# Expert blocks that finish their tokens themselves: the groups dealt in turn, rows added and scattered by slot

## The reference, cut to what matters

```
xn2 = rmsnorm(x, ffn_norm_w)                      # (1088, 1024)
grp = argmax(xn2 @ w_rg + b_rg)                   # one of 4 groups for each token
e   = (xn2 @ w_re + b_re)[grp]                    # 8 experts of that group
top_v, top_i = top_k(e, 2)                        # two experts, both of the one group
top_w = softmax(top_v) * softmax(group logits)[grp]
y = x + sum over the two of  top_w * ((silu(xn2 @ w_gate[e]) * (xn2 @ w_up[e])) @ w_down[e])
```

## Time and profile before

| | |
|---|---|
| median of three runs | 1497.39 us |
| profiled execution, span from first to last instruction | 1493.6 us |
| PE, DVE, ACT, POOL busy in the span | 95%, 67%, 49%, 14% |
| block loop, from the first turn of x to the last down product | 865.6 to 1455.6 us |
| one step of the loop | 18.02 us |
| tail, from the last down product to the end | 38 us |
| moved by DMA | 347.40 MB, 394 GB/s within the loop |

### The profile page before, as it was taken

How to read it: one execution, slowest core, us unless ns; L and a number is a source line. 1 busy time by engine, 2 the same in 40 slices (tenths; PEclk the granted TensorE clock), 3 DMA queues, 4 the chain that set the end, 5 groups by cost and what they waited for, 6 DMA issues and landing times.

```text
span 1493.6 us, 21566 instructions
## 1 busy us (share of the span) xinstructions
PE 1415.8 (95%) x8064; PEld 1198.3 (80%) x8064; DVE 1001.7 (67%) x1342; ACT 726.6 (49%) x862; POOL 210.4 (14%) x243
## 2 busy tenths in 40 slices
PE   7999999999999998999999889999999999999990
PEld 7899999989999998899888666777777777777760
DVE  4422321167666667776566688888888888888875
ACT  6421121144444445423211157777777777777760
POOL 2600000021111111000200040231111111111024
PEclk9999999999999999999999799999999999999995
DMA  6346323244333324658721389999999999999948
GB/s 200 120 152 212 119 80 70 75 136 129 122 115 112 109 68 119 196 172 251 284 83 42 133 325 380 374 378 400 392 389 395 389 388 397 396 396 395 363 137 310
DMA packets 135911, 347.40 MB, mean 233 GB/s; under 512 B 13784, under 2 KB 92060, under 8 KB 110176
## 3 DMA queue, kind: packets, MB, share of 16 engines
q1 hardware_dynamic: 125688, 312.32, 58.0%
q0 software_dynamic: 6048, 21.50, 4.7%
q10 hardware_dynamic: 4120, 12.85, 2.2%
HBM read 292.34 MB, written 55.28 MB: 233 GB/s over the span
## 4 chain that ended last, share of the span: by engine, by line
PE 45%; DVE 3%; DMA 2%; ACT 1%; POOL 1%; issue 1%; POOLq 0%; ACTq 0%; DVEq 0%
PE xt_ey L2595 4%; PE xt_ey L2596 4%; PE xt_ey L2597 4%; PE y_h_up L2574 4%; PE y_h_up L2573 4%; PE y_h_up L2575 4%; PE logits_gate L2573 2%; PE logits_gate L2575 2%; PE logits_gate L2574 2%; PE ranks_gate L2573 2%; PE ranks_gate L2575 2%; PE ranks_gate L2574 2%; PE y_x L2562 2%; DVE e_w_lo L2454 1%; PE y_x L2119 1%; PE y_h_up L2119 1%
## 5 line engine op out<-in xcount | busy, mean ns | idle before, releaser
L2454 DVE TENSOR_TENSOR e_w_lo<-mixed,e_w_hi 128x2048 fp32r<-128x2048 f32 x64 | 145.8, 2296 | 0.5 <-ACT e_w_hi L2387 0.5
L2454 DVE TENSOR_TENSOR e_w_lo<-w_out,e_w_hi 128x2048 fp32r<-128x2048 f32 x64 | 143.6, 2285 | 2.9 <-ACT e_w_hi L2387 2.9
L1008 PE MATMUL gate_banks<-f_hi,wg_hi 128*128 128x364 f32 (+1 forms) x376 | 126.8, 337 | 0.9 <-DVE wg_lo L876 0.4
L2387 ACT CAST e_w_hi<-mixed 128x2048 fp32r<-128x2048 f32 x62 | 117.0, 1913 | 14.0 <-ACT e_y_rows L2408 8.9
L1009 PE MATMUL gate_banks<-f_lo,wg_hi 128*128 128x364 f32 (+1 forms) x376 | 123.5, 328 | 0.0
L1010 PE MATMUL gate_banks<-f_hi,wg_lo 128*128 128x364 f32 (+1 forms) x376 | 123.4, 328 | 0.0
L2387 ACT CAST e_w_hi<-w_out 128x2048 fp32r<-128x2048 f32 x64 | 121.9, 1906 | 0.6 <-ACT e_y_rows L2408 0.6
L2595 PE MATMUL xt_ey<-e_w_hi,e_hT_hi 128*96 128x512 f32 x256 | 102.8, 402 | 4.2 <-DVE e_w_lo L2454 3.9
L2314 POOL CAST idx<-token_of_slot 96x1 uint32 (+1 forms) x30 | 48.6, 1620 | 402.0 <-PE y_x L2562 368.7
L2596 PE MATMUL xt_ey<-e_w_lo,e_hT_hi 128*96 128x512 f32 x256 | 101.5, 396 | 0.0
L2573 PE MATMUL y_h_up<-e_w_hi,e_x_hi 128*96 128x512 f32 x256 | 100.8, 394 | 0.8 <-DVE e_w_lo L2454 0.8
(11 more groups left out here) (634 smaller groups left out, 3604.7 us busy)
## 6 DMA issues: line engine op xcount, KB each, us to landing
w_out<-in_w_down_e SPq DMA_DIRECT2D x64, 1024.0 KB, 9.1
mixed<-in_w_gate_e SPq DMA_DIRECT2D x32, 1024.0 KB, 8.7
mixed<-in_w_up_e SPq DMA_DIRECT2D x32, 1024.0 KB, 9.4
w_gate<-in_w_gate_e SPq DMA_DIRECT2D x32, 1024.0 KB, 8.1
w_up<-in_w_up_e SPq DMA_DIRECT2D x32, 1024.0 KB, 8.7
expert_rows<-e_y_rows ACTq DMA_DIRECT2D x32, 384.0 KB, 7.3
proj<-mixed SPq DMA_DIRECT2D x8, 1408.0 KB, 5.6
w_ring<-in_w_in SPq DMA_DIRECT2D x7, 1408.0 KB, 10.7
```

Of the source, the lines that this page charges most:

```text
L1008: pe.matmul(bank, wg_hi[j][:, k, :], hi, start=(k == 0), stop=False)
L2387: act.copy(hi(i, step, j), raw(i, u, j)).then_inc(hi_ready[i], 1)
L2454: dve.tensor_tensor(lo(i, u, j), raw(i, u, j), hi(i, step, j).bitcast(F32), ALU.subtract).then_inc(lo_ready[i], 1)
```

## The change

The experts' order is changed, and each block finishes its rows.

- **Order.** Blocks 0 to 31 deal the four groups in turn: block b runs expert 8 (b mod 4) + b div 4.
- **Before the loop.** `route` also stores `x2` to a scratch `x2d` and, as a first value, to the outputs. It builds a weight for each slot (`weight_of`) with a second set of 18 small products. POOL clears the four row buffers. The column of `token_of` holds 16384 in empty slots, and the indirect DMAs skip such rows (`bounds_check`).
- **Facts.** DVE's `facts` works out for each of the 2176 rows ten numbers (which table its second operand is in, and where its result goes), in 51 small instructions in place of the 18 of `choices_in_order`. POOL scatters them in 18 indirect DMAs to `slot_info` and reads it back as `slot_table`. The extra blocks' tokens come from there, and `choice` and `labels` are gone.
- **Each block.** Before its rows are done, POOL has gathered into `y_rows` either the token's other, already computed row (`group_rows`) or its residual (`x2d`). DVE then writes weight x product + `y_rows` (`summed`), in place of ACT's copy. POOL scatters the result by slot to `group_rows`, or to the prompt's or the sample's output.
- **Last blocks.** From block 30 on POOL works block after block: it lets the writes of block b-1 land, then reads the output's own rows back as the second operand of block b.
- **Tail.** The gathers, the adds and the stores after the last block are gone.
- **Early.** The zeros stored in the projection stage go to the new tables, and one more DMA fills `slot_info`.

The core of the diff:

```diff
@@ facts for each row, on DVE (the middle is left out)
+    def facts(dve):
+        own = Own(dve, order_own)
+        L = own.link
+        dve.wait_ge(R.ordered, 1)
...
+        dve.tensor_scalar(general, pos, FIRST_GENERAL - 0.5, None, ALU.is_gt)
+        L(dve.scalar_tensor_tensor(R.info_at, slot, float(MAXB), pos, ALU.mult, ALU.add))
...
+        dve.tensor_copy(R.info[:, :, 0:WEIGHT], F[:, :, 0:WEIGHT]).then_inc(R.facts_known, 1)
@@ route, on SP
             sp.dma_start(a["xh2"][t * P:t * P + r, :], xh[u][:r]).then_inc(stored[u], 16)
+            sp.dma_start(a["x2d"][t * P:t * P + r, :], R.x2[:r, t, :]).then_inc(R.x2_stored, 16)
+            to = a["y_sample"].rearrange("b t d -> (b t) d") if r == TS else a["y_prompt"][0, t * P:t * P + r, :]
+            sp.dma_start(to, R.x2[:r, t, :]).then_inc(R.y_begun, 16)
@@ experts, on POOL
         def gather(b, u):
+            pool.wait_ge(s["xT_full"], b - 1)
+            pool.wait_ge(s["xT_full"], 1)
             pool.tensor_copy(idx[u][:], R.token_of[:, bass.ds(b, 1)]).then_inc(s["idx_ready"], 1)
             pool.wait_ge(s["idx_ready"], b - 1)
             pool.sem_inc(s["idx_seen"], 1)
-            pool.indirect_dma_start(xb[u][:], None, a["xh2"], bass.IndirectOffsetOnAxis(ap=idx[u][:, 0:1], axis=0)).then_inc(xb_loaded[u], 16)
+            get(xb[u][:], a["xh2"], idx[u][:, 0:1], T).then_inc(xb_loaded[u], 16)
+        def rows_out(b, u, between=lambda: None):
+            pool.wait_ge(y_stored, 16 * (b - NG))
+            pool.sem_inc(s["idx_seen"], 1)
+            put(u, Y_ROW, a["y_prompt"][0], TP).then_inc(y_stored, 16)
+            between()
+            pool.wait_ge(s_stored, 16 * (b - NG))
+            pool.sem_inc(s["idx_seen"], 1)
+            put(u, SAMPLE_ROW, ys, TS).then_inc(s_stored, 16)
+        def out(b, v, between):
+            pool.wait_ge(s["y_out"], b + 1)
+            pool.sem_inc(s["idx_seen"], 1)
+            put(v % 2, OWN_ROW, group_rows[v], GROUP).then_inc(rows_stored[v], 16)
+            rows_out(b, v % 2, between)
+        def rows_landed(b):
+            pool.wait_ge(y_stored, 16 * (b - NG + 1))
+            pool.sem_inc(s["idx_seen"], 1)
+            pool.wait_ge(s_stored, 16 * (b - NG + 1))
+            pool.sem_inc(s["idx_seen"], 1)
+        def rest(b, v, q):
+            u, w = v % 2, (v + 2) % NG
+            pool.wait_ge(rows_stored[w], 16 * (q + (v >= 2)))
+            pool.sem_inc(s["idx_seen"], 1)
+            pool.wait_ge(rows_stored[v], 16 * q)
+            pool.sem_inc(s["idx_seen"], 1)
+            if not isinstance(b, int) or b > NG + 1:
+                rows_landed(b - 2)
+            fields_of(b, u)
+            get(yb[u][:], group_rows[v], fields[u][:, OTHER_ROW:OTHER_ROW + 1], GROUP).then_inc(rest_loaded[u], 16)
+        def residual(v, q):
+            u = v % 2
+            pool.wait_ge(rest_loaded[u], 64 * q + 32 * (v // 2) - 16)
+            pool.sem_inc(s["idx_seen"], 1)
+            get(yb[u][:], a["x2d"], fields[u][:, X2_ROW:X2_ROW + 1], T).then_inc(rest_loaded[u], 16)
...
+        def around(b, v, q):
+            out(b - 2, (v + 2) % NG, lambda: residual((v - 1) % NG, q if v else q - 1))
+            gather(b + 2, v % 2)
+            rest(b, v, q)
...
+        with pool.Fori(FIRST_GENERAL // 2, more + 1) as tt:
+            for u in range(2):
+                b = 2 * tt + u
+                rows_landed(b - 2)
+                fields_of(b, u)
+                get(yb[u][:], first_rows, fields[u][:, FIRST_ROW:FIRST_ROW + 1], NG * SLOTS).then_inc(first_loaded, 16)
+                gather(b + 2, u)
...
+                pool.wait_ge(s["y_out"], b)
+                rows_out(b - 1, 1 - u)
+                rows_landed(b - 1)
+                get(yb[u][:], a["y_prompt"][0], fields[u][:, Y_BEFORE:Y_BEFORE + 1], TP).then_inc(rest_loaded[u], 16)
+                pool.wait_ge(rest_loaded[u], 32 * tt - 16)
+                get(yb[u][:], ys, fields[u][:, SAMPLE_BEFORE:SAMPLE_BEFORE + 1], TS).then_inc(rest_loaded[u], 16)
+        end = 2 * more + 1
+        pool.wait_ge(s["y_out"], end + 1)
+        rows_out(end, 1)
@@ experts, on ACT
-            if not first:
-                down_out(b - 2, u, tt - 1)
@@ experts, on DVE
+        def summed(b, u, tt):
+            dve.wait_ge(done[DOWN], 2 * b + 2)
+            dve.wait_ge(rest_loaded[u], 16 if isinstance(tt, int) and tt == 0 else 32 * tt)
+            dve.scalar_tensor_tensor(yb[u][:], Y[:SLOTS, :], R.weight_of[:, bass.ds(b, 1)], yb[u][:], ALU.mult, ALU.add).then_inc(s["y_out"], 1)
@@ experts, on PE
             if not first:
-                pe.wait_ge(s["y_act"], b)
+                pe.wait_ge(s["y_out"], b)
```

More of the change, by code:

```diff
@@ L2614, in step @@
             down(b - 1, 1 - u, u, first)
-            hidden(UP, b, u, 0, Up)
-            if choice is not None:
-                labels(choice)
-            hidden(UP, b, u, 1, Up)
+            for j in range(2):
+                hidden(UP, b, u, j, Up)
         turn(0, 0, 0, True)
```

430 lines of the change are left out of this document (252 added, 178 removed).

## The result

The changed kernel takes 1667.08 us (median of 6 runs, 1653.16 to 1672.69) against 1496.56 us (6 runs): ratio 1.1132, 95% interval 1.1085 to 1.1179. In the profiled execution the span is 1655.1 us, 161.5 more than before.

What follows compares the result with a forecast made beforehand. PE bounds the kernel, busy throughout at 18.02 us a step. 1493.6 + 7.6 (before the loop) + 72 (loop) - 16 (tail) = 1557.2 us of span, median 1561.0 us, 4.2% slower; range 1489 to 1640.

Steps and rivals of the forecast that it cites:

- The marks: Signs in the loop: steps of 20 us and more, `summed` waiting for transfers into `y_rows`, POOL busy above 60%.
- POOL's work and the blocking: In the block loop: 6.0 us of POOL instructions, and eight readers waiting 1.22 us each behind DVE, 9.8 us a block.
- The raises: On POOL in the loop: each semaphore raise costs 0.61 us, nine a block, 5.5 us.
- rival 3: Loop: the landings of row transfers pace it at 21.5 us a step, 1565 us in all, whatever DVE does; chance 0.10.
- Rivals 1 and 2: Loop: 1, POOL fits, steps 18.02 us, 1489 us, chance 0.17; 2, let in behind every piece, 19.3 us, 1511 us, 0.12.
- Bytes at nothing: In the loop: 1.6 MB more, 4 us at 394 GB/s if unhidden, counted as 0 since PE waits for no weight.
- Before the loop: Ahead of the steady loop: `facts` +7.0, `choice` and `labels` gone -3.7, `experts_out` +0.8, scatters of facts +3; sum +7.6 us.
- the 3.7 us for `choice` and `labels`: Early blocks: with `choice` and `labels` gone, two long steps (19.92 us between blocks 4 and 5) return to 18.02, -3.7 us.
- The tail: From block 30 on: a serial chain replaces the gathers, adds and stores after the last product, -16 us (-21 to -6).
- The last link: In the tail, from `summed` of block 30 to that of block 31: one serial link of 18.8 us.
- The first link: In the tail, from `summed` of block 29 to that of block 30, beginning with the scatter to y: 18.8 us.
- the forecast's loop term: Block 6 to block 29: POOL's round makes steps 21.3 us instead of 18.02, +72 us (22 to 153).

Runs made afterwards that it cites:

- a1: The changed kernel with DVE's low pieces computed without their second SBUF operand (low halves of the weights wrong): 1552.5 us, ratio 1.0378.
- c4: The changed kernel without copies in blocks 6 to 29, semaphore raises of blocks 2 to 29 gone too: 1616.9 us, against 1616.8 with raises.
- b1: The changed kernel with one-operand low pieces on DVE and four y buffers in place of two: 1537.5 us, ratio 1.0299.
- e1: b1 with the gathers of the other rows and x2's rows in blocks 4 to 29 replaced by 64-byte transfers: 1477.7 us, ratio 0.9891.
- b4: Changed kernel: blocks 6-29 without copies, four y buffers, x2 gather earlier, block 4's x gather behind tenth facts scatter, last blocks' copies behind gathers: 1612.3 us.

## Why the prediction was wrong, point by point

- **Direction and mechanism.** Slower, since POOL's round of indirect DMAs does not fit beside DVE: right. The marks were there: 24 us a step, idle time ahead of `summed` put down to transfers into `y_rows`, POOL at 63%.
- **POOL's work and the blocking.** 6.0 us of work were forecast; where nothing blocks (a1) a round takes 6.2. Blocked, at P = 21.3, it would be 9.8 x 18.02 / 21.3 = 8.3 us; found 9.1. That this term comes out near is luck. Readers arriving at any time would wait 1.22 us each; in fact one waits 6.4 us in every round and the others under 1. The prediction's average has no room for arrivals that DVE's own run is tied to.
- **The raises: the step that failed first.** 0.61 us each, 5.5 us a block, from 0.80 against 0.19 us in the earlier trace rows. But the 0.19 stood behind the wait for the first of two copies, long over. Behind a bare wait for a copy just issued (`first_at`, in the changed kernel) it is 0.78 too:

```profile
865.81 2.32 POOL L2391 DMA_INDIRECT y_rows<-x2d,first_at  x1 [0.78 <-issue]
```

  Two scatters with a wait and a raise between them stand 0.30 us apart, as do two scatters of facts with neither, and c4 shows no gain. Forecast 7.0 us for raises and waits, measured 3.2.
- **The landings: the step that failed worst.** The sum had none; they stood in rival 3 as a pace of their own (21.5 us), to hold *instead of* the blocking. They come one behind the other in the same round: 5.8 us. The two are not rivals but terms of one sum: 6.0 + 9.1 + 3.2 + 5.8. Against the forecast's round of 21.3 us the landings add 5.8 and the blocking 0.8, and the raises take off 3.8, so two errors partly cancel. The 2.7 us that are left make 65 us over 24 steps, nearly all that the forecast missed in the loop (135.6 against 72). Rivals 1 and 2, with steps of 18.02 and 19.3 us, are out by the 24.0.
- **Bytes at nothing.** As the changed kernel runs, right: at 24 us a step the DMA share is 0.84. But under POOL's round lies a floor of 20.4 us, which the argument (1.6 MB at 394 GB/s, "PE waits for no weight now") did not see. A price for gathered rows was needed, and the lead of the weights, not the wait, to say what was free. `summed` on DVE and the copy taken from ACT cost nothing where nothing else holds the loop: the steps of 18.0 us in b1 and e1 have both.
- **Before the loop, +7.6 forecast, +18.5 measured.** `facts` is right: PE waits 5.98 us ahead of block 1's gate where it waited 1.44, and block 2 comes 7.5 us late, 1.2 of them from before block 0. What failed is the 18 scatters of facts at 3 us:

```profile
886.88 2.80 POOL L2465 DMA_INDIRECT slot_info<-slot_facts,info_at  x1 [12.86 <-DVE slot_facts L1846]
...
935.99 1.89 POOL L2465 DMA_INDIRECT slot_info<-slot_facts,info_at  x1 [0.30 <-issue]
...
940.10 1.02 POOL L2391 DMA_INDIRECT x_rows<-xh,idx  x1 [0.90 <-POOL idx L2401]
```

  From the first to the last they take 51 us (3.6 of them for block 3's copy and gather), not 40, since DVE blocks them: without the second operand (a1) it is 25 us, and block 4 comes 19.2 us behind block 3. Here block 4's gather of x stands behind all of them, and its step takes 30.7 us where it took 19.9. Moving that gather ahead (b4) only handed the wait to block 5. Of the 3.7 us for `choice` and `labels` nothing shows: the step from block 4 to 5 takes 20.1 us, where it took 19.9.
- **The tail, -16 forecast, +7.5 measured from block 29 on.** The last link and the end are as forecast: 17.6 us between the last two sums (18.8), 9.5 us from the last to the end (9.1):

```profile
1595.60 1.28 DVE L2632 SCALAR_TENSOR_TENSOR y_rows<-xt_ey,weight_of_slot,y_rows 96x1024 f32<-96x1024 f32 x1 [5.11 <-DMA y_rows<-x2d,slot_fields]
...
1625.44 1.28 DVE L2632 SCALAR_TENSOR_TENSOR y_rows<-xt_ey,weight_of_slot,y_rows 96x1024 f32<-96x1024 f32 x1 [16.49 <-DMA y_rows<-y_sample,slot_fields]
...
1644.30 1.28 DVE L2632 SCALAR_TENSOR_TENSOR y_rows<-xt_ey,weight_of_slot,y_rows 96x1024 f32<-96x1024 f32 x1 [10.51 <-DMA y_rows<-y_sample,slot_fields]
```

  The first link is the miss: 28.6 us for 18.8, and it began 5.1 us late. The forecast began it with the scatter to y. In the program the wait for block 28's landings, the copy of fields and the gather of first rows stand ahead of that scatter, and the copy took 12.4 us. In b4, without that copy, the link is still 25.8 us, since the landing and the gather remain. Another 9.3 us are the two slow steps from block 29 to 31, which the forecast's loop term left out. From the last product to the end it is 16.7 us, where 22 were forecast and 38 were before: the tail is shorter, and what is lost lies ahead of it.

## What to carry to other kernels

When work moves to the queue engine, write out one round of it as a chain: every instruction, every landing it waits for, and which engine starts running at the moment of each release. Blocking and landings add up. An instruction released by the same event as a busy neighbour, or by one that always lands a little behind it, meets that neighbour every time, so price it at the neighbour's run (6.6 us here) and not at an average (1.2). A transfer that hides is not free: read the issue-to-landing time of the stream it shares the engines with over the loop, because a lead that shrinks by 0.7 us a step is a stall that has not arrived yet.
